# Eight of the twelve modulation tiles that ride in the first projection move into the first attention

## The reference

```python
c_lat, c_con = silu(c), silu(c_ctx)
m_lat = split(c_lat @ w_mod[0] + b_mod[0], 6)    # six vectors of 1024: 48 tiles of 128
m_ctx = split(c_con @ w_mod[0] + b_mod[0], 6)    # the same weights, the context's condition
h = rms_norm(x, g_pre_mix[0]) * (1 + m[1]) + m[0]            # m: m_lat or m_ctx
q, k, v = project(h, attn_w_qkv)                 # 12 tiles of 128 columns; q, k of latents turned (rope)
o = softmax_with_sink(q @ k.T, windowed) @ v     # 16 heads, 4 key heads, blocks of 128 queries
x = x + m[2] * rms_norm(o @ attn_w_o, g_post_mix[0])
f = relu(modulate(x, g_pre_mlp[0], m[3], m[4]) @ w_mlp_in) ** 2 @ w_mlp_out
x = x + m[5] * rms_norm(f, g_post_mlp[0])
```

## Time and profile before

| | us |
|---|---|
| median of 3 runs | 2666.02 |
| lowest and highest | 2663.15, 2666.35 |
| the profiled execution's own time | 2661.2 |
| its span in the trace | 2659.2 |
| PE busy | 2456.0 |
| DVE busy | 1689.5 |
| ACT busy | 1088.2 |

### The profile page before, as it was taken

One profiled execution on the slowest core, in us unless ns is written; L12 is line 12 of the kernel. 1 busy time (PEld: TensorE's weight loads), 2 busy tenths in 40 slices (PEclk: granted clock), 3 DMA queues, 4 the chain that ended last, 5 costly groups with the idle time before them and its releaser, 6 DMA issues. The chain is left out here.

```text
span 2659.2 us, 32740 instructions
## 1 busy us (share of the span) xinstructions
PE 2456.0 (92%) x12252; PEld 2029.1 (76%) x12252; DVE 1689.5 (64%) x2738; ACT 1088.2 (41%) x1739; POOL 94.3 (4%) x111
## 2 busy tenths in 40 slices
PE   6969899899999998899998899998889999899998
PEld 5865558699999997687776788887766667677776
DVE  7667778775646466655553634446347997569994
ACT  4424443431212133423333422334446663377773
POOL 0000000000000000000000000000001330020000
PEclk8989999899999999999999999998999999999999
DMA  7220004133323332011111222222211222159993
GB/s 254 89 85 1 0 1 166 49 127 127 127 96 127 103 127 87 17 48 48 42 39 48 71 96 100 99 96 79 76 64 44 72 68 71 41 200 343 342 338 137
DMA packets 78131, 275.62 MB, mean 104 GB/s; under 512 B 8800, under 2 KB 9312, under 8 KB 77856
## 3 DMA queue, kind: packets, MB, share of 16 engines
q1 hardware_dynamic: 74016, 265.74, 28.6%
q10 hardware_dynamic: 3968, 7.88, 1.0%
HBM read 271.49 MB, written 2.10 MB: 103 GB/s over the span
## 5 line engine op out<-in xcount | busy, mean ns | idle before, releaser
L638 PE MATMUL DP<-HH,WL 128*128 128x384 f32 (+2 forms) x1408 | 517.7, 368 | 28.9 <-DVE WL L631 21.8
L640 PE MATMUL DP<-HL,WH 128*128 128x384 f32 (+2 forms) x1408 | 504.3, 358 | 0.0
L639 PE MATMUL DP<-HH,WH 128*128 128x384 f32 (+2 forms) x1408 | 504.3, 358 | 0.0
L631 DVE TENSOR_TENSOR WL<-RAW,WH 128x1024 fp32r<-128x1024 f32 x230 | 280.9, 1224 | 217.4 <-ACT WH L604 210.8
L638 PE MATMUL DP<-A,WL 128*128 128x384 f32 (+2 forms) x1072 | 382.0, 356 | 22.6 <-issue 8.3
L639 PE MATMUL DP<-A,WH 128*128 128x384 f32 (+2 forms) x1072 | 378.9, 353 | 0.0
L640 PE MATMUL DP<-A,WH 128*128 128x384 f32 (+2 forms) x1072 | 378.6, 353 | 0.0
L604 ACT ACTIVATE WH<-RAW 128x1024 fp32r<-128x1024 f32 x230 | 241.2, 1051 | 291.5 <-PE DP L640 211.8
L638 PEld LDWEIGHTS DP<-HH,WL 128*128 128x128 f32 x1408 | 267.5, 190 | 67.8 <-DVE WL L631 32.6
L639 PEld LDWEIGHTS DP<-HH,WH 128*128 128x128 f32 x1408 | 267.4, 190 | 29.4 <-issue 5.5
L640 PEld LDWEIGHTS DP<-HL,WH 128*128 128x128 f32 x1408 | 267.1, 190 | 25.5
(11 more groups left out here) (416 smaller groups left out, 3885.1 us busy)
## 6 DMA issues: line engine op xcount, KB each, us to landing
RAW<-in_stream SPq DMA_DIRECT2D x326, 512.0 KB, 3.3
MRAW<-in_stream SPq DMA_DIRECT2D x168, 512.0 KB, 5.4
MATS<-in_ssm ACTq DMA_DIRECT2D x16, 256.0 KB, 2.6
X<-in_x SPq DMA_DIRECT2D x8, 384.0 KB, 9.9
BW<-in_rel ACTq DMA_DIRECT2D x4, 512.0 KB, 3.4
out<-X SPq DMA_DIRECT2D x8, 256.0 KB, 2.0
COND<-in_cond SPq DMA_DIRECT2D x1, 1024.0 KB, 4.9
CONST<-in_const SPq DMA_DIRECT2D x1, 256.0 KB, 4.9
```

The lines of the kernel that those rows point to most:

```text
L631: dve.tensor_tensor(WL[:, w, :], RAW[:, nxt.u % RING, :], WH[:, w, :].bitcast(F32), ALU.subtract).then_inc(raw_done[nxt.u % RING], 1)
L638: pe.matmul(out, al, bh, start=first, stop=False)
L639: pe.matmul(out, ah, bh, start=False, stop=False)
L640: return pe.matmul(out, ah, bl, start=False, stop=last)
```

## The change

rides_after gives one tile each to t = 0 to 3 and none to 4 to 7, which had two each. A new function, rides_within, gives one tile each to the attention steps 1, 3, ..., 15. In the stream, those eight tiles stand behind the last projection tile. VectorE works one behind maxima(n+2) of these steps, as the last thing of the step. mod_add_bias for the twelve values moves behind the attention loop, ahead of the last normalise. The work as a whole, and its DMAs, stay the same in number and size.

```diff
 def rides_after(t):
 
-    return (1 if t < 4 else 2) if t < 8 else 0
+    return 1 if t < 4 else 0
+
+
+def rides_within(n):
+
+    return 1 if n % 2 and n < 16 else 0
@@ schedule()
         for _ in range(rides_after(t)):
+            mod(0, next(rides))
+    for n in range(24):
+        for _ in range(rides_within(n)):
             mod(0, next(rides))
     dense("attn_w_o", 0)
@@ VectorE's program
             rope(9)
             rope_low(9)
-            mod_add_bias(dve, 12, lambda n, o=0: slice(o + 16, o + 16 + n))
+
             def maxima(n, g, b, near):
@@
                 if n + 2 < len(WORK):
                     maxima(*WORK[n + 2][0:4])
+                mods(rides_within(n))
+            mod_add_bias(dve, 12, lambda n, o=0: slice(o + 16, o + 16 + n))
             normalise(n)
             mixed_low(n, g, b)
             split_low(dve, nxt)
```

## The result

The changed kernel took 2675.8 us as the median of 5 runs (2674.6 to 2679.5) against 2666.0 us (5 runs, 2663.2 to 2669.8): ratio 1.0041, 95% interval 1.0027 to 1.0055. Run again later as a control: 2678.0 against 2666.7 us, 1.0046 (1.0029 to 1.0063). It is slower by some 0.4%, +10 to +11 us, where +11.1 us was forecast. Its profiled execution took 2679.0 us, with a span of 2677.2 us.

What follows compares the result with a forecast made beforehand. VectorE was taken to set the pace in projection steps with two tiles, and a ring of engine waits, with VectorE on the path, to bound the attention. -14.8 + 20.6 + 0.3 + 5.0 = +11.1 us gave 2677.1 us, range 2669 to 2686.

Steps and rivals of the forecast that it cites:

- Part 1: Projection: eight tiles leave steps 4 to 7, so the value projection starts 14.8 us earlier (bounds 13.2 and 16.4).
- The walk: Projection: rotations followed 9.18 us apart to the value projection's first product, at 159.35 in place of 174.12.
- Rival (d): Projection: ScalarE's copies hold TensorE, so the gain is 10 us, not 14.8; 2681.9 us, chance 0.10.
- Part 2: Attention: eight tiles at 2.71 us each, less 0.37 us of slack in three steps, cost 20.6 us.
- The bound of 19.6: Attention: lower bound of the tiles' cost, with 0.2 us of unlisted slack in each of the five other steps.
- Part 4: Attention: longer TensorE stalls bring five falls of its clock at 1.0 us each, 5.0 us (bounds 0 and 12.8).
- Part 3: Ahead of the last normalise: two bias additions moved there cost between 0 and 0.3 us, taken as 0.3.
- Rival (a): Attention: VectorE's 56 us of idle hide the tiles, so they cost zero; 2651.2 us, chance 0.08.
- Rival (b): Attention: stalls too short for any fall of the clock; +6.1 us, 2672.1 us, chance 0.20.
- Rival (c): Attention: the clock falls behind each of the eight stalls; +18.9 us, 2684.9 us, chance 0.12.

Runs made afterwards that it cites:

- another parity: The changed kernel with its eight attention tiles behind the maxima of steps 0, 2, ..., 14 instead of 1, 3, ..., 15: 2668.0 us, ratio 1.0006.
- the kernel with cut products: The changed kernel with its products in the attention on 8 of 1024 columns, all loads and waits kept: 2651.5 us, ratio 0.9943.
- the shorter fill: The changed kernel with 29, 17 or 20 useless TensorE products in its stalls, instead of 40, 24 or 28: 2668.9 us, ratio 1.0017.

## Why the prediction was right, step by step

**Right in sign, size and mechanism, with luck in how near it came.** 2677.1 us forecast, 2675.8 and 2678.0 measured; +11.1 us forecast, +9.8 and +11.3 measured.

- *Part 1, the projection:* -14.8 forecast, -14.7 at equal start. The idle before the value projection is 6.21 us, as expected. The walk's sum gives 159.3, not 159.35, which changes nothing. Rival (d) falls: the gain came whole, and no rotation from 116.82 to the value projection has an idle for ScalarE's copy in front of it, where the one at 161.49 had 2.60 us before. The test that I gave, a first product near 159.4 and no later than 162, would have been failed by the letter (162.58), since it took the start for fixed; measured from the projection's start it holds. The clock was at 0.50 behind the shorter idle too, as expected.
- *Part 2, the tiles:* +20.6 forecast, 19.0 measured (the control too). The term was a little too large: 2.71 us is the spacing of two tiles in the projection, and at the attention's place a tile adds 2.53 us, as worked out above. Times 8, less 3 x 0.37, that makes 19.1. The bound of 19.6 was thus too high. The six-block period with three tiles was to grow by 7.5 us or more; from 206.25 to 267.96 are 61.71 us, 10.4 more than 51.27; without the two falls of the clock in it 7.1 us, a little under what I had named. The stalls of steps 2, 8 and 14 are 3.16 us, where 3.3 were forecast; the five others are 1.92 and 2.16, where I had said 2.3 to 2.7.
- *Part 4, the clock:* +5.0 forecast, 7.8 measured. The number of falls, five, was right, and so were the three long stalls. The price was the term that I mis-sized: 1.0 us taken, 1.55 us measured on average. Slices of 0.25 us show that the stretch at 1.2 GHz was mis-sized too. I had counted 3.3 us; it was 3.4 us in steps 7, 9 and 13 and 6.8 us in steps 3 and 15 (from 218.6, before the stall ended, to 225.3). The price doesn't grow with it: 1.66 us for both long stretches, 1.65 and 1.62 us in steps 7 and 13, where half of 3.4 us, 1.7, is all that TensorE could lose. It was less, 1.18 us, in step 9, where the clock (third last, as in the slices above) fell only 2 us behind the end of the stall at 281.12:

```profile
282.00:283.00 1.00, 0.56 (x4) 0.41 (x3) 1.00 (x2) 0.00 (x0) 0.00 (x0) 1.00 0.00 0
283.00:284.00 1.00, 1.00 (x5) 0.92 (x5) 0.80 (x3) 0.00 (x0) 0.00 (x0) 0.68 0.00 0
```

  In the control step 9 has a long stretch and costs 1.57, and step 15 the late one and costs 1.19. So directly behind a stall half rate costs nearly all that TensorE loses in the first 3.4 us; there the sharing with VectorE's maxima, for which I had taken off 0.6 us, is not seen. What hides the later part of the long stretches no run shows.
- The two errors, -1.6 and +2.8, took part of each other away. The profiled execution's 4.8 us under the median were carried over as they stood, and medians and stages differ by up to 5 us in the experiments. That the forecast came to within 1.3 us of both medians is in part luck.
- The Trainium skill (TensorE: Matmul & The Clock Gate, section HAM oscillation) has recurring waits throttle TensorE anew each time. The runs agree for the stalls of 3.16 and 2.16 us, behind which the clock fell in every period. Those of 1.92 us recur too and brought no fall; the waits of the section's own example are longer, so this is a limit of what it says of this kernel and no contradiction.
- *Part 3, the bias:* between 0.2 and 0.3 us, as forecast:

```profile
419.44 0.24 DVE L791 TENSOR_TENSOR MOD<-MODT,VECS 128x12 f32<-128x12 f32 x2
419.72 0.72 DVE L2529 STREAM_TRANSPOSE RCT<-XP 64x512 f32<-64x512 f32 x1
```

- *Rival (a),* that 56 us of idle hide 21.7 us of work, falls at the place of the tiles: before rows_low of the even-numbered steps, where they land, there was next to no slack. With another parity 7 of 20 us did hide, and in halves placed at the slack nearly all. The idle was usable, but not from where the change puts the tiles.
- *Rival (b),* no falls, is contradicted by the five falls. What it would have given was nearly made with the extra products, though with two other falls: 1.0017 of 2666.0 is 2670.6, where it said 2672.1. *Rival (c),* a fall behind each stall, is contradicted by the three stalls of 1.92 us without one.
- The loads cost nothing that can be seen, as was said: the attention with extra products and no loads was as long as that with them.

## What to carry to other kernels

In this kernel, work added to VectorE's list cost its length less the slack in front of the next thing that another engine waits for, at the very place where it stands. Read that slack step by step in the time line; the engine's busy share says nothing about it. Here the same eight tiles cost 19 us behind the maxima of odd steps and 13 behind those of even ones, while four tiles cut in halves, at steps with 1.2 us of slack, cost 1. And a stall that such work causes can have a second price, TensorE's clock, which here came to two fifths of the first.

## What the runs showed of the hardware that was not expected

- Products without any use kept TensorE's granted clock at 2.4 GHz across stalls of 2.2 to 3.2 us, and four steps got back 1.2 to 1.7 us each. Each takes some 0.12 us (40 in 4.98 us), and where they ran 0.55 to 1.1 us past the stall the gain was nearly gone (the whole time 2677.7 us, against 2678.0 without them).
- The length of the stall alone doesn't decide. Behind stalls of 3.15 and 2.16 us the clock fell each time, as behind 3.05 and 2.04 us in the kernel with extra products on VectorE; behind 1.92 us it didn't in six cases (two profiles), nor behind 1.81 us in three. But the kinds of step differ as well as the stalls, and single falls also came behind 1.04 us (steps 3 and 15 of the kernel with cut products, not step 9) and where the idle in front was no longer than in the kernel before, 0.86 us or less: in steps 6 and 9 with five tiles in the value projection, in step 21 with the other parity, and in steps 12 and 21 with the shorter fill. They cost 0.8 to 1.2 us each, and no run here shows what brings them.
- A fall's price depends on when it comes more than on how long it lasts: 1.6 to 1.8 us for 3.4 and for 6.8 us at 1.2 GHz around or directly behind a stall's end, 1.2 us for 3.4 us that began 2 us later (step 9 of the changed kernel, step 15 of the control, step 6 of the other parity).
- The start of the kernel, up to the projection's first product, scatters by 4 us between executions (53.9 to 58.5 us). In the control VectorE waited 3.86 and 2.07 us for two of the first modulation tiles to land, where it waited 1.64 us and none before. The part behind the attention scatters by 11 us (2253.8 to 2264.9 us). Together that is as large as the effects looked for here, while the projection and the attention of the changed kernel repeat to 0.1 us; a single fall of the clock moves the attention by about 1 us.
